# HGRN scores: levels 0 and 1 taken into one product of 192 query columns per chunk

## What is computed

```python
def hgrn2_mix(h, s0, w_in, lb, norm_w, w_o):
    q, fl, iv, g = jnp.split((h @ w_in).astype(jnp.float32), 4, axis=-1)
    f = lb + (1.0 - lb) * jax.nn.sigmoid(fl)
    log_f, k = jnp.log(f), 1.0 - f
    def step(s, blk):                       # blocks of HG_BLOCK steps, per head
        bcum = jnp.cumsum(lfc, axis=2)
        decay = where(mask, exp(bcum_t - bcum_s), 0)
        scores = einsum('bhtk,bhsk,bhtsk->bhts', qc, kc, decay)
        o = scores @ ic + (qc * exp(bcum)) @ s
        s = exp(b_last) * s + (kc * exp(b_last - bcum))^T @ ic
        return s, o
    o = o * rsqrt(mean(o * o) + EPS) * norm_w * silu(g)
    return o @ w_o
```

## Time and profile before

| | us |
|---|---|
| median of 3 runs | 2759.84 (2758.64 to 2762.13) |
| the profiled execution | 2757.03 |
| its span, first to last instruction | 2755.2 |

### The profile page before, as it was taken

The page is one execution under the profiler, slowest core; times in us unless marked ns, Lnnn a source line. Parts: engine busy times, 40 slices in busy tenths (PEclk is TensorE's granted clock), DMA queues, the critical chain, the costliest instruction groups (busy, mean ns, idle before and its releaser), DMA issues.

```text
span 2755.2 us, 41981 instructions
## 1 busy us (share of the span) xinstructions
PE 2683.2 (97%) x17508; PEld 2639.6 (96%) x17508; DVE 2132.8 (77%) x2389; ACT 840.7 (31%) x1259; POOL 1269.8 (46%) x913
## 2 busy tenths in 40 slices
PE   8999998999999999999999999999899999999998
PEld 8999898999999999999999999989899999999998
DVE  8996768999999855566777777796899999985555
ACT  3000534444444300031221221233444444430002
POOL 5222365777777523253212122116577777752324
PEclk9999999999999999999999999999999999999999
DMA  5221142222212422231111111104221222242222
GB/s 155 54 64 35 33 153 82 74 79 75 73 72 73 169 96 94 92 115 47 40 48 47 40 48 41 47 25 153 79 78 73 80 73 73 73 170 97 94 91 77
DMA packets 132365, 219.09 MB, mean 80 GB/s; under 512 B 67536, under 2 KB 85968, under 8 KB 132176
## 3 DMA queue, kind: packets, MB, share of 16 engines
q1 hardware_dynamic: 50928, 121.91, 13.1%
q10 hardware_dynamic: 81248, 94.49, 10.2%
HBM read 164.52 MB, written 51.86 MB: 79 GB/s over the span
## 4 chain that ended last, share of the span: by engine, by line
PE 89%; DVE 6%; POOL 2%; issue 1%; ACT 1%; DMA 0%; DVEq 0%; ACTq 0%; SPq 0%; POOLq 0%
PE BANKS L935 34%; PE BANKS L895 27%; PE BANKS L1201 14%; PE BANKS L1475 3%; PE BANKS L1022 3%; PE BANKS L1257 2%; PE BANKS L1245 1%; PE BANKS L1163 1%; POOL OPS L761 1%; DVE HGA L2644 1%; DVE XL L2126 1%; PE BANKS L1312 1%; PE BANKS L1331 1%; PE BANKS L1302 1%; PE BANKS L1318 0%
## 5 line engine op out<-in xcount | busy, mean ns | idle before, releaser
L731 POOL TENSOR_TENSOR SMALL<-WRAW 128x1 f32<-128x1 f32 x108 | 28.8, 267 | 1099.8 <-PE BANKS L895 524.1
L935 PE MATMUL BANKS<-XB_A,OPS 128*128 128x288 f32 x3432 | 515.7, 299 | 20.5 <-issue 20.2
L935 PEld LDWEIGHTS BANKS<-XB_A,OPS 128*128 128x128 f32 x3432 | 478.3, 191 | 25.4 <-issue 22.9
L935 PE MATMUL BANKS<-XB_B,OPS 128*128 128x288 f32 x2904 | 438.8, 297 | 0.3 <-DVE XB_B L2398 0.3
L895 PE MATMUL BANKS<-GHL,WH 128*128 128x384 f32 x2100 | 421.9, 335 | 6.3 <-POOL WL L734 3.6
L935 PEld LDWEIGHTS BANKS<-XB_B,OPS 128*128 128x128 f32 x2904 | 405.1, 189 | 0.7 <-DVE XB_B L2398 0.5
L2352 DVE TENSOR_TENSOR X<-BANKS,X 128x1152 f32<-128x1152 f32 x152 | 206.2, 1356 | 237.5 <-PE BANKS L895 210.9
L895 PEld LDWEIGHTS BANKS<-GHL,WH 128*128 128x128 f32 x2100 | 369.6, 188 | 7.7 <-issue 4.0
L2537 DVE SCALAR_TENSOR_TENSOR C<-U,HGA,C 128x1168 f32<-128x1168 f32 x176 | 273.9, 1576 | 35.6 <-ACT C L1846 34.0
L734 POOL TENSOR_TENSOR WL<-WRAW,WH 128x1024 fp32r<-128x1024 f32 x108 | 267.8, 2480 | 8.6
L761 POOL TENSOR_TENSOR OPS<-TMP,OPS 128x512 fp32r<-128x512 f32 x176 | 236.5, 1353 | 66.9 <-ACT OPS L1770 66.7
(11 more groups left out here) (294 smaller groups left out, 4993.4 us busy)
## 6 DMA issues: line engine op xcount, KB each, us to landing
WRAW<-in_w SPq DMA_DIRECT2D x100, 512.0 KB, 3.4
RAW<-in_w SPq DMA_DIRECT2D x88, 512.0 KB, 4.3
GR<-g_kept ACTq DMA_DIRECT2D x22, 1152.0 KB, 5.2
g_kept<-C ACTq DMA_DIRECT2D x44, 512.0 KB, 2.6
x_kept<-X ACTq DMA_DIRECT2D x24, 576.0 KB, 2.7
XB_BF<-x_kept SPq DMA_DIRECT2D x16, 576.0 KB, 7.2
X<-in_x SPq DMA_DIRECT2D x8, 576.0 KB, 8.9
X<-in_x ACTq DMA_DIRECT2D x8, 576.0 KB, 7.1
```

Of the source, the lines that this page charges most:

```text
L935: ins = nc.tensor.matmul(out[:, cols], w[:, a, p, :], x[:, b, cols], start=s in OPENS and p == 0 and q == 0, stop=p == PAIRS - 1 and q == ...
```

## The change

Level 0 joins level 1 as the other levels are joined. For each pair of neighbouring columns the widened operand has three: the even query and the odd query as they are (level 0) and the odd query times its own gate (level 1). ScalarE copies the first two (640 and 512 elements), VectorE makes the third (320 and 256). `scores`, `own`, `pick` and `first_level` go; the product `own` made, QFS times FG, is now made in `first_raised`, after J0B. The masked copies are three per part, over single columns: PSUM is read with a step of three elements, the mask and the scores with a step of two. J0B lies in the narrow place 1. On TensorE the blocks move among the slices; VectorE widens ahead of `totals` (in head 7 behind it) and both thirds of the reciprocals now stand ahead of the picks.

```diff
-JOINED = (2, 4, 6)
+JOINED = (0, 2, 4, 6)
+SHORT_JOIN = STREAM_LEVELS - 1
...
-NARROW = ("SUM", "J2B", "J4B", "J6B", "NS")
+NARROW = ("SUM", "J0B", "J2B", "J4B", "J6B", "NS")
...
             first_values()
-            scores(0, 0)
-            part("G", 0, 0, 4)
-            scores(1, 0)
-            part("G", 0, 4, KD)
+            part("G", 0, 0, 1)
+            joined(0, "A", 0)
+            part("G", 0, 1, 2)
+            joined(0, "B", 0)
+            part("G", 0, 2, KD)
...
                     sums(h - 1)
-                    part("G", h, 2, 3)
-                    scores(0, h)
-                    part("G", h, 3, 5)
-                    scores(1, h)
+                    part("G", h, 2, 4)
+                    joined(0, "A", h)
+                    part("G", h, 4, 5)
+                    joined(0, "B", h)
                     part("G", h, 5, KD)
...
             part("V", h + 1, 3, 4)
-            scores(0, h)
-            part("V", h + 1, 4, 6)
-            scores(1, h)
-            part("V", h + 1, 6, KD)
+            joined(0, "A", h)
+            part("V", h + 1, 4, 5)
+            joined(0, "B", h)
+            part("V", h + 1, 5, KD)
...
             def widened(l, h):                     # ScalarE
+                if l == 0:
+                    emptied_big(act, "Q", h)
+                    if h == 0:
+                        act.wait_ge(kept, 16 * KD)
+                    elif h == HEADS - 1:
+                        emptied_small(act, "O", h - 1)
+                    for part in "AB":
+                        c0, c1 = part_chunks(l, part)
+                        q = QFS[h % 2][:, c0 * P:c1 * P].rearrange("p (g f) -> p g f", f=2)
+                        w = wide(h, part)[:, 0:(c1 - c0) * WIDE].rearrange("p (g f) -> p g f", f=3)[:, :, 0:2]
+                        A(w, q, ACT.Copy).then_inc(q_wide, 1)
+                    return
...
             sigmoid_f(0)
+            widened(0, 0)
             for h in range(HEADS):
+                if h == HEADS - 1:
+                    widened(0, h)
                 if h:
                     root(h - 1)
...
                     states_out(h)
+                    if h < HEADS - 2:
+                        widened(0, h + 1)
...
+            def first_widened(h):                  # VectorE
+
+                emptied_big(dve, "Q", h)
+                mine()
...
+                for part in "AB":
+                    c0, c1 = part_chunks(0, part)
+                    q, f = [v[:, c0 * P:c1 * P].rearrange("p (g f) -> p g f", f=2)[:, :, 1:2] for v in (QFS[h % 2], FG)]
+                    x = wide(h, part)[:, 0:(c1 - c0) * WIDE].rearrange("p (g f) -> p g f", f=3)[:, :, 2:3]
+                    V.tensor_tensor(x, q, f, ALU.mult).then_inc(kq, 1)
+
+            def first_raised(h):
+
+                full_small(dve, "J0B", h)
+                dc.inc(V.tensor_tensor(QFS[h % 2], QFS[h % 2], FG, ALU.mult))
+                raised(1, h).then_inc(q_rdy, 1)
+                widened(2, h)
+
+            def first_picks(part, h):
+
+                full_small(dve, f"J0{part}", h)
+                if h:
+                    emptied_small(dve, f"J6{part}", h - 1)
...
+                def one(f, plane, l):
+
+                    k = MASK[:, l, :].rearrange("p (c g f) -> p c g f", c=1, f=2)[:, :, :, f].broadcast_to([P, n, P // 2])
+                    return V.copy_predicated(to[:, :, :, f], k, data[:, :, :, plane])
+
+                mine()
+                dc.inc(one(0, 0, 0))
+                dc.inc(one(1, 1, 0))
+                mine()
+                one(1, 2, 1).then_inc(s_free[small_place(f"J0{part}")], 1)
...
             for h in range(HEADS):
+                if 0 < h < HEADS - 1:
+                    first_widened(h)
                 if h:
                     totals()
+                if h == HEADS - 1:
+                    first_widened(h)
                 if 0 < h < HEADS - 1:
                     dc.inc(gated(h - 1))
                 if h:
                     inverse(h - 1, 0)
-                own(h)
-                if h:
                     inverse(h - 1, 1)
-                first_level(h)
+                first_picks("A", h)
+                first_raised(h)
+                first_picks("B", h)
```

More of the change, by code:

```diff
@@ L136 @@
     _early = _h == HEADS - 2
-    SMALLS += [(_n, _h) for _n in (("VT",) if _early else ()) + ("L0", "L1", "J2A", "J2B")]
+    SMALLS += [(_n, _h) for _n in (("VT",) if _early else ()) + ("J0A", "J0B", "J2A", "J2B")]
     SMALLS += [(_n, _h) for _n in (() if _early else ("VT",)) + ("J4A", "J4B", "J6A", "J6B")]
@@ L464, in part_chunks @@
                 return 0, A_CHUNKS
-            return A_CHUNKS, TCH if l < JOINED[1] else PCH
+            return A_CHUNKS, TCH if l < SHORT_JOIN else PCH
         def wide(h, part):
@@ L1232, in take @@
                     emptied_big(pe, "Q", 0)
[L1234 to L1246, removed]
             def joined(l, part, h):
                 n = 2 * JOINED.index(l) + (part == "B")
-                pe.wait_ge(kq, h * (LEVELS + 1) + 3 + n)
+                pe.wait_ge(kq, h * (LEVELS + 2) + 2 + n)
                 pe.wait_ge(q_wide, 2 * len(JOINED) * h + n + 1)
@@ L1258, in joined @@
                                            start=True, stop=True)
-                if (l, part) == (JOINED[1], "B"):
+                if (l, part) == (SHORT_JOIN, "B"):
                     a = slice(PCH * P, T)
@@ L1404, in _ @@
             sums(h - 1)
[L1405 to L1408, removed]
+            part("G", h - 1, 2, 4)
+            joined(0, "A", h)
+            part("G", h - 1, 4, 5)
+            joined(0, "B", h)
             part("G", h - 1, 5, KD)
@@ L2663, in totals @@
                     dc.inc(V.tensor_tensor(TOT[:, a:a + w], b[:, :, 0], b[:, :, 1], ALU.mult))
[L2665 to L2682, removed]
             def raised(l, h):
@@ L2728, in widened @@
                                     ).then_inc(kq, 1)
-            def first_level(h):
-                full_small(dve, "L1", h)
+            def first_widened(h):
+                emptied_big(dve, "Q", h)
+                mine()
+                if h == 0:
+                    dve.wait_ge(kept, 16 * KD)
+                elif h == HEADS - 1:
+                    emptied_small(dve, "O", h - 1)
+                for part in "AB":
[6 more added lines that the diff above has]
+                dc.inc(V.tensor_tensor(QFS[h % 2], QFS[h % 2], FG, ALU.mult))
                 raised(1, h).then_inc(q_rdy, 1)
                 widened(2, h)
-                pick(1, h)
+            def first_picks(part, h):
+                full_small(dve, f"J0{part}", h)
+                if h:
+                    emptied_small(dve, f"J6{part}", h - 1)
+                c0, c1 = part_chunks(0, part)
+                n = c1 - c0
+                data = joined_out(0, part, 0, n).rearrange("p (c w) -> p c w", w=2 * P)[:, :, 0:WIDE].rearrange(
+                    "p c (g f) -> p c g f", f=3)
+                to = SC[:, c0:c1, :].rearrange("p c (g f) -> p c g f", f=2)
+                def one(f, plane, l):
[6 more added lines that the diff above has]
+                one(1, 2, 1).then_inc(s_free[small_place(f"J0{part}")], 1)
             def joined_raised(l, h):
@@ L2855, in _ @@
             projected("Q", 0, QFS[0])
-            dc.inc(V.memset(SC, 0.0))
             forget(0)
             key(0)
+            first_widened(0)
+            dc.inc(V.memset(SC, 0.0))
             totals()
@@ L2878, in _ @@
                     projected("G", h - 1, GATE)
-                emptied_small(dve, "L1", h)
+                emptied_small(dve, "J0A", h)
+                emptied_small(dve, "J0B", h)
                 picks(2, "A", h)
```

16 lines of the change are left out of this document (3 added, 13 removed).

## The result

| | before | after |
|---|---|---|
| median (lowest to highest), runs | 2758.36 us (2751.93 to 2762.13), 16 | 2764.9 us (2761.11 to 2768.69), 16 |
| after / before | | 1.0026, 95% interval 1.002 to 1.0033 |
| span of the profiled execution | 2755.2 us | 2762.9 us |
| granted clock of the span | 0.992 | 0.991 |

What follows compares the result with a forecast made beforehand. TensorE was taken to bound the kernel, with VectorE about 0.5 us behind it in the mixer heads. +6.8 (heads 1 to 5 and 7) - 1.2 (head 6) + 0.5 (head 0) = +6.1 us on 2759.84 gave 2765.9 us, range 2752 to 2780.

Steps and rivals of the forecast that it cites:

- What bounds the head: Head 2 of the mixer: TensorE bounds it, VectorE has about 0.5 us of slack ahead of G's scaling.
- TensorE's part: Each mixer head: shorter level 0 products, J0A to 1.48 and J0B to 1.18 us, save TensorE 1.2 us a head.
- The picks: Six new masked copies on VectorE: priced like runs of 2, 2.38 us for the first three, 1.92 for the others.
- the two other prices: Rival costs of the six copies: 1.35 and 1.14 us (chance 0.32), or 2.98 and 2.45 us (chance 0.20).
- The path, heads 1 to 5 and 7: VectorE's work up to G's scaling delays V's start from 1434.09 to 1435.23: 1.14 us a head, +6.8 us for six.
- Head 6: The second reciprocal fills VectorE's idle time, and F starts at 1741.35 against 1742.51: -1.2 us.
- Head 0: G's first slice waits 1.7 us for V(0)'s scaling, against 1.2 us saved by shorter products: +0.5 us.
- At nothing: VectorE's widening products behind GpSimd's weight split and ScalarE's two copies fall into existing waits and cost nothing.
- The first: Rival: masked copies run at the pace of long runs, 1.35 and 1.14 us; -5.3 us, 2754.5 us; chance 0.32.
- The second: Rival: each single element pays a break's surplus, copies 2.98 and 2.45 us; +13.6 us, 2773.4 us; chance 0.20.
- the third: Rival: another cover fails (widening, ScalarE's copies) or one more holds; a few microseconds either way; chance 0.08.
- The sum: Whole kernel: +6.8 - 1.2 + 0.5 = +6.1 us on the three-run median 2759.84, giving 2765.9 us.

Runs made afterwards that it cites:

- experiment 8: Kernel before the change with level 1's masked copy made twice, 1.4 us more VectorE work ahead of G's scaling; median 2766.18 us, 1.0034 of before.
- experiments 4: Changed kernel with level 0's masked copies over whole rows, two dense stores per part instead of three stepped ones; median 2756.34 us, 0.9993 of before.
- experiment 5: Changed kernel with the second part's level 0 masked copies moved behind G's scaling (V's in head 6); median 2756.16 us, 0.9996 of before.
- experiment 7: Changed kernel with whole-row masked copies, G's scaling ahead of the second part's copies, and head 0's J0A ahead of G's first slice; median 2747.17 us, 0.9965 of before.
- experiment 1: Changed kernel with PSUM read, mask or store of its masked copies made dense by head; 320 elements take 0.50 to 0.52 us with dense stores, otherwise 0.87 to 0.93.
- experiment 2: Changed kernel with level 0's copies storing runs of 1 to 64 columns by head, and a plain copy in head 6; one run 2757.17 us.
- Experiment 6: Changed kernel with only head 0's order changed, J0A ahead of G's first slice; one run 2764.03 us, V(0) to sums 89.09 us against 90.67.

## Why the prediction was right, point by point

**What bounds the head.** Right. TensorE bounded it, with VectorE 0.5 us behind, and that slack decided the case: experiment 8 spends it without touching TensorE and makes the kernel slower too, though there the place of L1 in PSUM sets the price; experiments 4 and 5 shorten VectorE's way to the scaling and get the time of before, and in experiment 7 TensorE's saving appears whole.

**TensorE's part.** J0A at 1.48 us: 1.49. J0B at 1.18: 1.16. The slice behind J0B, at 1426.39 with sums at 1417.23, so 9.16 behind them: 1426.76 - 1417.57 = 9.19. The 1.2 us of saving: 1.16 in experiment 7.

**The picks.** Priced at 2.38 and 1.92 us, measured 2.32 and 1.87. The row was well chosen, the reason that went with it was wrong: "broken reads are what the new form has in common with level 2". Both have broken stores in common as well, and those are what costs (experiment 1). No row could tell the two apart, since level 2 breaks both. That the price of a run of two could be carried over to single elements unchanged was not something the forecast knew. That was luck: it holds because runs of one and of two lie on one level (experiment 2), and the forecast gave the two other prices 0.52 between them.

**The path, heads 1 to 5 and 7.** Scaling of G foretold at 1433.73 - 1417.23 = 16.50 us behind the sums, measured 16.41; V at 18.00, measured 17.94; +1.04 and +1.09 a head for +1.14. One wait wasn't in the sum: J2A stands 0.30 us for its widened queries (L2703). It costs nothing, since V waits for the scaling anyway; experiment 5 leaves this wait as it is and still starts V 1.87 us nearer to the sums.

**Head 6.** -1.18 for -1.2. The second reciprocal went into VectorE's idle time, J2A's wait of 1.24 us is gone, and in its place F's first slice stands behind the scaling. Timeline of TensorE, head 6, after (answers to the earlier trace rows):

```profile
1742.93 1.79 PE L1244 MATMUL BANKS<-X,HGA 128*128 128x192 f32 x10
...
1745.90 0.76 PE L1202 MATMUL BANKS<-XH,WH 128*128 128x384 f32 x3 [1.18 <-DVE HGA L2644]
```

**Head 0.** +0.60 for +0.5. G's first slice starts 14.19 us behind the start of V(0), where L0 started at 12.48: 1.71 us later, as foretold (1.54 of them appear as idle time). From there to J2A the change saves 1.08 and not 1.2, since G's eight slices together take 12.84 us in the new order and 12.70 in the old. Experiment 6 takes the wait out.

**At nothing.** The widening products were held behind GpSimd's split as described (3.14 us for two, from 1410.67), the seven totals behind them shrank from 4.52 to 2.47, and VectorE's next step still waited 0.57 us for ScalarE at 1416.74. ScalarE's two copies fell into its wait. Timelines of GpSimd and ScalarE, head 2, after (answers to the earlier trace rows):

```profile
1410.64 2.36 POOL L735 TENSOR_TENSOR WL<-WRAW,WH 128x1024 fp32r<-128x1024 f32 x1
...
1410.67 1.29 ACT L2011 ACTIVATE X<-HGA 128x640 f32<-128x640 f32 x2 [11.15 <-DVE HGA L2644]
```

**The rivals.** The first needed picks at the pace of long runs. With those it comes true head for head, once the clock in head 7 is allowed for (experiments 1 and 2), but the stores kept the two at 4.2 us together, beyond its 3.2. The second needed a surplus for each break; none is seen. Of the third, a cover that fails, nothing is seen either.

**The sum.** +5.7 us in the mixer for +6.1, and a median of 2764.9 us for 2765.9. The medians' +6.5 against the +5.7 of the heads lies within the interval of the ratio, 5.5 to 9.1 us, and the 0.8 between them was not traced. The forecast lies above the median although its difference is too small, because the three runs that it started from had a median 1.5 us above that of all 16.

## What to carry to other kernels

A shorter product is worth what the step that frees its successor's bank lets through: read first how long the engine of that step pauses ahead of it. With 0.5 us of pause, a saving of 1.2 us on TensorE became a loss of 1.04, and moving later what that step doesn't need brought it back. In copies under a mask write whole rows, or runs of at least four fp32 elements; how PSUM and the mask were read mattered in none of these kernels.

## What the runs showed of the hardware

- A predicated copy from PSUM into SBUF takes 0.87 to 0.93 us for 320 fp32 elements in 128 partitions when it stores runs of 1 or 2 elements, and 0.49 to 0.52 for runs of 4 and more. For 160 elements it is 0.54 against 0.34 in the median, so the price goes by the element: (0.88 - 0.54) / 160, about 2.1 ns, against (0.51 - 0.34) / 160, about 1.1 ns, as an estimate from these medians. Runs of three, other types and other alignments weren't tried, and why the mask makes the store slow stays open. The Trainium skill (Advanced Engine Details and Errata, SBUF Cachelines) asks for at least two hits on a line of 16 bytes; stores in runs of two have them and are slow under the mask (884 ns), unmasked stores at a step of two have them too and are not (492 ns). The rule doesn't tell the two apart.
- Reads of single PSUM elements at a step of three by VectorE cost nothing: 0.50 us for 320, as dense ones, in masked copies with dense stores, and 0.49 in plain ones.
- Idle time of 2.69 us on TensorE, in head 6 of the last experiment, was followed by some 6 us at the level of 1.2 GHz, which cost 3 us on top of the wait. The waits of 1.58, 1.54 and 1.18 us in the changed kernel were not: the granted clock is 1.00 throughout heads 0, 2 and 6 there. The length of the wait alone doesn't decide it: every profile has one of 1.71 or 1.72 us ahead of the last sums of head 7, and the clock fell to 0.50 in it in four (before, after, experiments 2 and 7; for 3.4 us in the first two, 6.8 in the others) and stayed at 1.00 in six.
